# RWKV scan in 64x64 blocks: each head's own 64 columns, on the diagonal quarters of the array

## Chip, core and metric

The program runs on one core of a Trainium2 chip. The metric is the device time of one launch in microseconds. The inputs and outputs are float32, and so is all arithmetic in the part that the change touches.

## What is computed

The program is a two-layer trunk over 256 context tokens and 1024 latent tokens of width 1024. The change is in the first layer's RWKV mixer: 8 heads of 64 channels, scanned over the tokens in both directions, context first.

```python
def delta_scan(s0, seq, dr, reverse):
    '''S <- S diag(w) - (S kk)(kk*a)^T + v k^T ; y = S r.  S: (B,H,Nv,Nk).'''
    def step(s, inp):
        r_t, w_t, k_t, v_t, kk_t, a_t = inp
        s_kk = jnp.einsum('bhvk,bhk->bhv', s, kk_t)
        s = (s * w_t[:, :, None, :] - s_kk[..., None] * (kk_t * a_t)[:, :, None, :]
             + v_t[..., None] * k_t[:, :, None, :])
        return s, jnp.einsum('bhvk,bhk->bhv', s, r_t)
    s_last, ys = lax.scan(step, s0, xs, reverse=reverse)
...
for dr, reverse in enumerate((False, True)):
    s_ctx, yc = delta_scan(s0, ctx, dr, reverse)
    _, yl = delta_scan(s_ctx, lat, dr, reverse)
```

## The kernel before

The 1280 tokens are cut into 20 chunks of 64, and the scan is done chunk by chunk. Inside a chunk the recurrence is a triangular system, whose 64x64 inverse is built by doubling: five levels, each of a product, a copy, a second product and a correction. Between chunks a 64x64 state per head is carried.

`rwkv_scan_phase` runs once for each pair of heads (j = 0 to 3). A pair fills the 128 partitions: head 0 in partitions 0 to 63, head 1 in 64 to 127. The inverse's matrices are kept 128 by 128, one block per head on the diagonal and zeros off it, so that one 128x128 product serves both heads; the cross terms that the products of keys leave are masked by `tri`. Some operands hold the two heads in flipped halves (`vflip`, and `BK` for head 1), so that one 128-row product gathers what it needs from an off-diagonal block. An operand `KR` holds kappa and r of each head beside zeros for the other head.

A pair has 10 rounds and a closing one. Round m does two things at once: it builds the inverses of its two chunks g = 0, 1 in both directions dr (`inv`), and it carries the state through the two chunks of round m-1 (`seq`). The order of the work on each engine is written out by hand. On TensorE (lines 1879 to 1916) it is: `turn_rows` (transposes of the keys, L1839), `right(0)`, `first_inverse` (L1848), `solve(0)`, `level_a(1)`, `outputs(0)`, `level_b(1)`, `level_a(2)`, `right(1)`, `level_b(2)`, `level_a(3)`, `solve(1)`, `level_b(3)`, `level_a(4)`, `outputs(1)`, `level_b(4)`, `level_a(5)`, `products(m+1)` (L1927, the keys' products of the next round), `level_b(5)`. `level_a(l)` is, for each g and dr, a transpose of X (L1863) and a product (L1866); `level_b(l)` is one product each (L1876). Between them VectorE copies Z (L2055) and corrects X (L2063), and ScalarE copies Y (L1955).

In pairs 0 to 2 `PairPrep` computes the next pair's keys in the same rounds: products L1486 to L1502 on TensorE, `unit_key`, `shift` and `scans` on VectorE, `keys` and `rows` on GpSimd, and tables and copies on ScalarE. The last pair has none of it.

SyncE issues all transfers. `stage(m)` loads a round's keys: for j over 0 three transfers per chunk and direction (L1716, L1717), for j = 0 five (L1721 to L1724). `BK` has one buffer, so that `stage(m)` waits for the transposes of round m-1; `KR` has three.

```python
sp.dma_start(KR[hp, m % 3, g, dr, :, h * CK:(h + 1) * CK], kb[j, dr, e, hp, 0:2, :]).then_inc(kr_in[g], 16)
sp.dma_start(BK[:, g, dr, :, :], kb[j, dr, e, :, 2:4, :]).then_inc(bk_in[g], 16)
...
nc.tensor.transpose(bankY[g][:, dr * P:(dr + 1) * P], X[:, g, dr, :], ident[:, :])
x = nc.tensor.matmul(to, Bm[:, g, dr, l, :], X[:, g, dr, :], start=True, stop=True)
```

Of the kernel before, what the change touches and what calls it, by code (L numbers as in the profile page):

```python
# [1395 lines left out]
class PairPrep:  # L1396
# [226 lines left out]
    def rows(self, pool, m):  # L1623
# [21 lines left out]
def rwkv_scan_phase(nc, sems, j, d, kr, bk, kb, last, vtok, srk, lora, projT, yout):  # L1645
# [7 lines left out]
    with ExitStack() as ctx:  # L1653
        s = Scope(nc, ctx, sems, f"rs{j}")
        ident, levels = s.sb("ident", [P, P]), s.sb("levels", [P, 6, P])
        tri, first = s.sb("tri", [P, 2, 2, 2, P]), s.sb("first", [P, 2, 2, P])
        BK = s.sb("BK", [P, 2, 2, 2, CK])
        KR = s.sb("KR", [P, 3, 2, 2, 2, P])
        vflip = s.sb("vflip", [P, NCK, HD])
        gm = s.sb("gm", [P, 2, 2, 2, 2, 2, P])  # L1660
# [40 lines left out]
        with nc.Block() as block:  # L1701
            @block.sync
            def _(sp):
                def stage(m):
# [1477 lines left out]
```

## Time and profile before

| | |
|---|---|
| median of 3 runs | 5291.36 us (5290.5 to 5294.35) |
| profiled execution, its own time | 5289.93 us |
| its span in the trace | 5288.0 us |
| four scans of head pairs, from 880 to about 2131 us | 331, 325, 326 and 269 us |
| in the third pair (1536 to 1862 us) busy: TensorE, VectorE, ScalarE, GpSimd | 255, 202, 144, 126 us |
| in the last pair (1862 to 2131 us) busy: the same | 228, 149, 74, 52 us |
| all that comes before and after the scans | 880 and 3157 us |

The scans take 1251 us of the span, and the change touches nothing else. Within a pair the rounds repeat: from the second on they are 27.9 us apart in pairs 0 to 2 and 23.7 us in the last one. A float32 product stands in the trace as two records of TensorE and two of its weight loads, a transpose as one of each.

### The profile page before, as it was taken

The numbers are of one execution on the slowest core, as the hardware profiler recorded it, in microseconds if no ns is written. First come the engines' busy times: TensorE is split into PE (matmuls) and PEld (weight loads), VectorE is DVE, ScalarE is ACT, GpSimd is POOL, SyncE is SP. The second block draws the span as 40 slices with busy tenths as digits, with TensorE's granted clock in tenths as the row PEclk, the third lists the DMA queues.
The fourth block names the chain that finished last, engine by engine and source line by source line (L and its number), as shares of the span: only waits on it lengthen the run. The fifth ranks groups of instructions, "written<-read, shape, count | busy, mean of one in ns | idle before, by whom it ended". The sixth has DMA issues, their size and how long they took to land. (4 is left out here: it accounts for less than half of the span.)

```text
span 5288.0 us, 69064 instructions
## 1 busy us (share of the span) xinstructions
PE 4090.6 (77%) x23906; PEld 2744.6 (52%) x23907; DVE 2109.5 (40%) x4441; ACT 1455.8 (28%) x3296; POOL 716.9 (14%) x1002
## 2 busy tenths in 40 slices
PE   4998982886868879285799994499899764799973
PEld 2886761775757878172233331389566452233321
DVE  3314545774747655525000002542577534000003
ACT  2213542553435523102111110211466511111111
POOL 0000000343434421301000001010000011000001
PEclk7999995998989989596899997699999886899996
DMA  7211001112111110327868997421300122478996
GB/s 288 71 67 46 8 17 45 44 40 58 48 50 43 38 48 17 115 99 252 310 255 310 375 396 290 159 92 61 129 10 11 55 82 92 184 307 342 394 427 228
DMA packets 292547, 780.17 MB, mean 148 GB/s; under 512 B 114276, under 2 KB 203128, under 8 KB 261592
## 3 DMA queue, kind: packets, MB, share of 16 engines
q1 hardware_dynamic: 239032, 645.96, 33.2%
q10 hardware_dynamic: 38736, 82.33, 4.1%
q0 software_dynamic: 14544, 48.79, 2.5%
q8 instruction: 143, 2.34, 0.2%
q14 instruction: 92, 0.75, 0.1%
HBM read 651.51 MB, written 117.60 MB: 145 GB/s over the span
## 5 line engine op out<-in xcount | busy, mean ns | idle before, releaser
L2862 PE MATMUL ex_bY<-ex_w,ex_aT 128*64 x880 | 389.1, 595 | 73.7 <-DVE ex_aT L2925 73.7
L2862 PE MATMUL ex_bG<-ex_w,ex_xT 128*64 x880 | 404.6, 614 | 39.3 <-SPq L2783 25.8
L2865 PE MATMUL ex_bG<-ex_w,ex_xT 128*64 128x512 f32 x880 | 404.6, 614 | 0.0
L2865 PE MATMUL ex_bY<-ex_w,ex_aT 128*64 128x512 f32 x880 | 389.4, 595 | 0.0
L2865 PE MATMUL ex_bU<-ex_w,ex_xT 128*64 128x512 f32 x880 | 386.6, 592 | 0.0
L2862 PE MATMUL ex_bU<-ex_w,ex_xT 128*64 x880 | 386.6, 592 | 0.0
L2923 DVE TENSOR_TENSOR ex_a<-ex_sg,ex_bU 128x512 f32<-128x512 f32 x55 | 37.8, 688 | 808.0 <-PE ex_bU L2865 808.0
L2862 PEld LDWEIGHTS ex_bG<-ex_w,ex_xT 128*64 128x64 f32 x880 | 123.9, 142 | 302.0 <-issue 302.0
L2862 PEld LDWEIGHTS ex_bY<-ex_w,ex_aT 128*64 128x64 f32 x880 | 116.0, 137 | 299.8 <-issue 299.8
L1022 DVE TENSOR_SCALAR_CACHE_REDUCE ad_p<-ad_S 128x512 f32<-128x512 f32 (+1 forms) x384 | 215.7, 600 | 100.5 <-PE ad_S L944 100.5
L2862 PEld LDWEIGHTS ex_bU<-ex_w,ex_xT 128*64 128x64 f32 x880 | 120.6, 137 | 247.5 <-issue 247.5
L1866 PE MATMUL rs_bankZ<-rs_X,rs_Bm 128*128 128x128 f32 x1280 | 225.3, 277 | 0.0
L1863 PE MATMUL rs_bankY<-rs_ident,rs_X 128*128 128x128 f32 x640 | 185.3, 289 | 43.5 <-DVE rs_Bm L2081 37.8
L1778 POOL TENSOR_TENSOR rs_Bm<-rs_gm,rs_levels 128x384 f32<-128x384 f32 x160 | 157.2, 1004 | 427.9 <-DVE rs_gm L2049 425.0
L1876 PE MATMUL rs_bankY<-rs_Z,rs_Y 128*128 128x128 f32 x1280 | 185.9, 288 | 37.2 <-DVE rs_Z L2055 37.1
L2896 ACT ACTIVATE ex_xT<-ex_tr 128x512 f32<-128x512 f32 x114 | 62.1, 594 | 546.4 <-PE ex_tr L2847 546.4
L2929 DVE COPY ex_y<-ex_bY 128x512 f32<-128x512 f32 x55 | 38.0, 692 | 434.4 <-PE ex_bY L2865 434.4
L1955 ACT ACTIVATE rs_Y<-rs_bankY 128x256 f32<-128x256 f32 x320 | 122.9, 384 | 318.2 <-PE rs_bankZ L1866 318.2
L944 PE MATMUL ad_S<-ad_K,ad_q 64*128 64x512 f32 (+1 forms) x768 | 193.6, 584 | 17.2 <-DMA ad_lqk<-in_od_lk 13.0
L1866 PEld LDWEIGHTS rs_bankZ<-rs_X,rs_Bm 128*128 128x128 f32 x1280 | 205.0, 200 | 0.0
L2063 DVE TENSOR_TENSOR rs_X<-rs_X,rs_bankY 128x256 f32<-128x256 f32 x320 | 134.3, 421 | 169.8 <-PE rs_bankY L1876 166.1
L969 PE MATMUL ad_acc<-ad_V,ad_pT 128*128 128x128 f32 x1280 | 186.9, 285 | 17.9 <-ACT ad_pT L1093 17.9
(435 smaller groups left out, 9736.1 us busy)
## 6 DMA issues: line engine op xcount, KB each, us to landing
ex_w<-in_moe_w_gate SPq DMA_DIRECT2D x64, 2048.0 KB, 11.8
ex_w<-in_moe_w_up SPq DMA_DIRECT2D x64, 2048.0 KB, 16.1
ex_w<-in_moe_w_down SPq DMA_DIRECT2D x64, 2048.0 KB, 15.3
yb_dram<-ex_y ACTq DMA_DIRECT2D x55, 512.0 KB
rt_mw<-in_mod_w SPq DMA_DIRECT2D x24, 1024.0 KB, 9.0
n_mw<-in_mod_w SPq DMA_DIRECT2D x16, 1024.0 KB, 7.5
kb_dram<-rs_pout SPq DMA_DIRECT2D x60, 256.0 KB, 2.5
p_w<-in_od_w_in SPq DMA_DIRECT2D x12, 1024.0 KB, 5.0
```

The lines of the kernel that those rows point to most:

```text
L944: x = nc.tensor.matmul(S[j % 2][c][:, 0:w], q[h, pair, t * P - q_from:(t + 1) * P - q_from], K[h, kmap(pair), a:a + w], start=True, stop=True)
L969: x = nc.tensor.matmul(acc[m % 2][:, c * HD:c * HD + VW], pT[:, g % 3, k * P:(k + 1) * P], V[:, kt, vc:vc + VW], start=kt == 0, stop=kt == ...
L1022: nc.vector.tensor_scalar(p[:, u, c, a:a + w], S[j % 2][c][:, 0:w], scale, None, ALU.mult, ALU.max, accum_out=top[:, u, c, i:i + 1]).then_ ...
L1778: x = nc.gpsimd.tensor_tensor(Bm[:, g, dr, 3:6, :], gm[:, par, g, dr, 0, 0:1, :].to_broadcast([P, 3, P]), levels[:, 3:6, :], ALU.mult)
L1863: nc.tensor.transpose(bankY[g][:, dr * P:(dr + 1) * P], X[:, g, dr, :], ident[:, :])
L1866: x = nc.tensor.matmul(to, Bm[:, g, dr, l, :], X[:, g, dr, :], start=True, stop=True)
L1876: x = nc.tensor.matmul(bankY[g][:, 256 + dr * P:256 + (dr + 1) * P], a[:, g, dr, :], b[:, g, dr, :], start=True, stop=True)
L1955: aa.did(f"X{g}" if l == 1 else f"Y{l}{g}", nc.scalar.activation(to[:, g, :, :], bankY[g][:, 0:256].rearrange("p (d t) -> p d t", d=2), AC ...
L2063: va.did(f"X{l}{g}", nc.vector.tensor_tensor(X[:, g, :, :], X[:, g, :, :], corr, ALU.subtract))
L2862: nc.tensor.matmul(bank[0:BR, :], stationary[:, k, 0:BR], w[:, ds(slot0 + (offset + k * n), 512)], start=k == 0, stop=k == tiles - 1)
L2865: m = nc.tensor.matmul(bank[BR:P, :], stationary[:, k, BR:P], w[:, at:at + 512], start=k == 0, stop=k == tiles - 1)
L2896: nc.scalar.activation(xT[:, 4 * b:4 * b + 4, :], tr[b][:, :].rearrange("p (k t) -> p k t", k=4), ACT.Copy).then_inc(xT_done, 1)
```

## The change

Each head now keeps only its own 64 columns. All matrices of the inverse are 64 columns wide over 128 partitions, one head above the other, and no zeros are stored. Each product is made of two halves, which stand on the diagonal quarters of the array: head 0 reads partitions 0 to 63 and writes PSUM partitions 0 to 63, head 1 reads and writes 64 to 127. The transposes become products with a unit matrix `eye`, two halves each; the transposes of the keys take four halves per chunk and direction instead of one instruction (beta and key apart, beta by minus `eye`). The element-wise operations on VectorE, ScalarE and GpSimd go over half the columns, and the masking operation over 512 in place of 1024. The flipped layouts go: `KR` and `BK` become one tile `KB` with three buffers, loaded by one transfer per chunk and direction (for j = 0 by two), and the first `stage` stands ahead of the constants. The memsets of `KR` and `btm` go. ScalarE's four half-partition operations per chunk after the transposes become one, and four half-partition operations of `rows` on GpSimd become two.

```diff
@@ PairPrep.rows
-        for h in range(2):
-            pool.wait_ge(self.parts, n + 1 + 2 * h)
-            g.tensor_tensor(self.out[h * HD:(h + 1) * HD, :, :, 2 + h, :], chunks(self.be, h), chunks(self.inv, h), ALU.mult).then_inc(self.parts, 1)
-            g.tensor_tensor(self.out[h * HD:(h + 1) * HD, :, :, 3 - h, :], chunks(self.kd, h), chunks(self.inv, h), ALU.mult).then_inc(self.parts, 1)
+        g.tensor_tensor(self.out[:, :, :, 2, :], chunks(self.be), chunks(self.inv), ALU.mult).then_inc(self.parts, 1)
+        g.tensor_tensor(self.out[:, :, :, 3, :], chunks(self.kd), chunks(self.inv), ALU.mult).then_inc(self.parts, 1)
@@ rwkv_scan_phase
-        KR = s.sb("KR", [P, 3, 2, 2, 2, P])
+        KB = s.sb("KB", [P, 3, 2, 2, 4, CK])
...
-        X, Y, Z = (s.sb(n, [P, 2, 2, P]) for n in "XYZ")
+        X, Y, Z = (s.sb(n, [P, 2, 2, HD]) for n in "XYZ")
@@ stage
+                    if m >= 3:
+                        pb.wait(sp, "d11", m - 3)
                     for g in GS:
-                        if m:
-                            pa.wait(sp, f"T{g}", m - 1)
-                        if m >= 3:
-                            pb.wait(sp, "d11", m - 3)
...
-                                sp.dma_start(BK[:, g, dr, :, :], kb[j, dr, e, :, 2:4, :]).then_inc(bk_in[g], 16)
+                                sp.dma_start(KB[:, m % 3, g, dr, :, :], kb[j, dr, e, :, :, :]).then_inc(kb_in[g][m % 3], 16)
...
+                stage(0)
+                for t, n in ((ident, "ident"), (levels, "levels"), (eye, "eye"), (tri, "tri"), (first, "first")):
                     sp.dma_start(t[:], d[n]).then_inc(c_in, 16)
-                sp.wait_ge(kr_clear, 1)
-                stage(0)
@@ TensorE
+                def halves(out, left, right, start=True, stop=True):
+
+                    for hp in HALVES:
+                        x = nc.tensor.matmul(out[hp], left[hp], right[hp], start=start, stop=stop)
+                    return x
...
-                            nc.tensor.matmul(bankS[dr][:, 0:HD], KR[:, q3, c, dr, 0, :], S[:, dr, :], start=True, stop=False)
+                            halves(bankS[dr][:, 0:HD], KB[:, q3, c, dr, 0, :], S[:, dr, :], stop=False)
...
-                                x = nc.tensor.transpose(bankY[g][:, dr * P:(dr + 1) * P], BK[:, g, dr, :, :].rearrange("p a t -> p (a t)"), ident[:, :])
+                                for a in range(2):
+                                    x = halves(bankY[g][:, (2 * dr + a) * HD:(2 * dr + a + 1) * HD], KB[:, m % 3, g, dr, 2 + a, :], eye[:, 1 - a, :])
...
-                                    nc.tensor.transpose(bankY[g][:, dr * P:(dr + 1) * P], X[:, g, dr, :], ident[:, :])
+                                    halves(bankY[g][:, dr * HD:(dr + 1) * HD], X[:, g, dr, :], eye[:, 0, :])
...
-                            x = nc.tensor.matmul(bankZ[g][:, dr * 256:(dr + 1) * 256], BK[:, g, dr, :, :].rearrange("p a t -> p (a t)"), KR[:, m % 3, g, dr, :, :], start=True, stop=True)
+                            for a in range(2):
+                                x = halves(bankZ[g][:, (2 * dr + a) * P:(2 * dr + a + 1) * P], KB[:, m % 3, g, dr, 2 + a, :], KB[:, m % 3, g, dr, 0:2, :].rearrange("p k t -> p (k t)"))
@@ ScalarE
-                            for h in range(2):
-                                hp, other = slice(h * HD, (h + 1) * HD), slice((1 - h) * HD, (2 - h) * HD)
-                                nc.scalar.activation(btm[hp, par, g, :, 0, hp], T[hp, :, hp], ACT.Copy, scale=-1.0)
-                                x = nc.scalar.activation(btm[hp, par, g, :, 1, other], T[hp, :, other], ACT.Copy)
-                            aa.did(f"bt{g}", x)
+                            aa.did(f"bt{g}", nc.scalar.activation(btm[:, par, g, :, :, :], bankY[g][:, 0:256].rearrange("p (d a t) -> p d a t", d=2, a=2), ACT.Copy))
@@ VectorE
-                nc.vector.memset(KR[:, :, :, :, :, :], 0.0).then_inc(kr_clear, 1)
...
-                        pair = bankZ[g][:, :].rearrange("p (k o t) -> p k o t", o=1, t=P).to_broadcast([P, 4, 2, P])
-                        va.did(f"gm{g}", nc.vector.tensor_tensor(gm[:, par, g, :, :, :, :].rearrange("p a b c t -> p (a b) c t"), pair,
-                                                                 tri[:, :, :, :, :].rearrange("p a b c t -> p (a b) c t"), ALU.mult))
+                        va.did(f"gm{g}", nc.vector.tensor_tensor(gm[:, par, g, :, :, :, :].rearrange("p a b c t -> p (a b c t)"), bankZ[g][:, :],
+                                                                 tri[:, :, :, :, :].rearrange("p a b c t -> p (a b c t)"), ALU.mult))
```

The remaining products of `right`, `solve`, `outputs` and the levels change in the same way, from one call of `matmul` to one of `halves`.

TensorE, second pair (rs1), one level of round 0: `level_b(1)` and `level_a(2)` of the kernel before. bankY and bankZ are the PSUM banks of chunk g, ident is the unit matrix.

```order
L1876 MATMUL rs1_bankY0<-rs1_Z,rs1_Y 128x128 x2
L1876 MATMUL rs1_bankY1<-rs1_Z,rs1_Y 128x128 x2
L1863 MATMUL rs1_bankY0<-rs1_ident,rs1_X 128x128
L1866 MATMUL rs1_bankZ0<-rs1_X,rs1_Bm 128x128
L1863 MATMUL rs1_bankY0<-rs1_ident,rs1_X 128x128
L1866 MATMUL rs1_bankZ0<-rs1_X,rs1_Bm 128x128
L1863 MATMUL rs1_bankY1<-rs1_ident,rs1_X 128x128
L1866 MATMUL rs1_bankZ1<-rs1_X,rs1_Bm 128x128
L1863 MATMUL rs1_bankY1<-rs1_ident,rs1_X 128x128
L1866 MATMUL rs1_bankZ1<-rs1_X,rs1_Bm 128x128
```

The same place after the change; all of them now stand under the line of `halves`, L1778.

```order
L1778 MATMUL rs1_bankY0<-rs1_Z,rs1_Y 64x64 x4
L1778 MATMUL rs1_bankY1<-rs1_Z,rs1_Y 64x64 x4
L1778 MATMUL rs1_bankY0<-rs1_eye,rs1_X 64x64 x2
L1778 MATMUL rs1_bankZ0<-rs1_X,rs1_Bm 64x64 x2
L1778 MATMUL rs1_bankY0<-rs1_eye,rs1_X 64x64 x2
L1778 MATMUL rs1_bankZ0<-rs1_X,rs1_Bm 64x64 x2
L1778 MATMUL rs1_bankY1<-rs1_eye,rs1_X 64x64 x2
L1778 MATMUL rs1_bankZ1<-rs1_X,rs1_Bm 64x64 x2
L1778 MATMUL rs1_bankY1<-rs1_eye,rs1_X 64x64 x2
L1778 MATMUL rs1_bankZ1<-rs1_X,rs1_Bm 64x64 x2
```

The order of the steps is the same; each instruction became two, of head 0 and then of head 1.

SyncE's queue at the start of the second pair, before the change.

```order
L1726 DMA rs1_ident<-in_ident 128x128
L1726 DMA rs1_levels<-in_levels 128x768
L1726 DMA rs1_tri<-in_tri 128x1024
L1726 DMA rs1_first<-in_first 128x512
L1716 DMA rs1_KR<-kb_dram 64x2x64 x2
L1717 DMA rs1_BK<-kb_dram 128x128
...
L1731 DMA rs1_vflip<-vtok 64x10x64 x4
```

And after it.

```order
L1709 DMA rs1_KB<-kb_dram 128x256 x4
L1715 DMA rs1_ident<-in_ident 128x128
L1715 DMA rs1_levels<-in_levels 128x384
L1715 DMA rs1_eye<-in_eye 128x128
L1715 DMA rs1_tri<-in_tri 128x512
L1715 DMA rs1_first<-in_first 128x256
L1718 DMA rs1_vch<-vtok 64x10x64 x4
```

The keys' transfers went from twelve (the pattern of three stands four times) to four, and moved ahead of the constants, which went from four to five; the 19 transfers of the preparation's constants follow in both.

## Rows read from the trace of the kernel before

**Rows 1.** Windows: length, PE, PEld, DVE, ACT, POOL busy, clock, DMA share, GB/s.
```profile
1645.70:1673.60 27.90, 24.18 (x191) 22.16 (x191) 19.74 (x47) 14.39 (x48) 12.11 (x20) 1.00 0.17 46
2064.70:2088.40 23.70, 22.08 (x177) 20.37 (x177) 14.32 (x35) 7.37 (x30) 5.01 (x8) 1.00 0.10 24
```

**Rows 2.** Timeline, third pair, TensorE: T, levels 2 to 5, products, next T.
```profile
1645.73 0.89 PE L1839 MATMUL rs_bankY<-rs_ident,rs_BK 128*128 128x128 f32 x4
...
1653.93 0.33 PE L1863 MATMUL rs_bankY<-rs_ident,rs_X 128*128 128x128 f32 x1 [0.85 <-DVE rs_Bm L2081]
...
1658.25 0.33 PE L1863 MATMUL rs_bankY<-rs_ident,rs_X 128*128 128x128 f32 x1
...
1662.21 0.33 PE L1863 MATMUL rs_bankY<-rs_ident,rs_X 128*128 128x128 f32 x1
...
1667.42 0.31 PE L1863 MATMUL rs_bankY<-rs_ident,rs_X 128*128 128x128 f32 x1
...
1669.81 1.97 PE L1927 MATMUL rs_bankZ<-rs_KR,rs_BK 128*128 128x256 f32 x8 [0.86 <-DVE rs_Z L2055]
...
1673.63 0.44 PE L1839 MATMUL rs_bankY<-rs_ident,rs_BK 128*128 128x128 f32 x2
```

**Rows 3.** Timeline, last pair, TensorE: T, level 2, level 4, level 5.
```profile
2064.67 0.89 PE L1839 MATMUL rs_bankY<-rs_ident,rs_BK 128*128 128x128 f32 x4
...
2072.87 0.33 PE L1863 MATMUL rs_bankY<-rs_ident,rs_X 128*128 128x128 f32 x1 [0.85 <-DVE rs_Bm L2081]
...
2079.23 0.33 PE L1863 MATMUL rs_bankY<-rs_ident,rs_X 128*128 128x128 f32 x1
...
2083.97 0.33 PE L1863 MATMUL rs_bankY<-rs_ident,rs_X 128*128 128x128 f32 x1
```

**Rows 4.** Timeline, TensorE without waits: transposes and products of level 4, then outputs(1).
```profile
1662.60 0.27 PE L1863 MATMUL rs_bankY<-rs_ident,rs_X 128*128 128x128 f32 x1
...
1662.93 0.27 PE L1863 MATMUL rs_bankY<-rs_ident,rs_X 128*128 128x128 f32 x1
...
1664.88 0.39 PE L1830 MATMUL rs_bankS<-rs_vflip,rs_btm 128*128 128x64 f32 x2
...
1665.55 0.39 PE L1831 MATMUL rs_bankS<-rs_U,rs_btm 128*128 128x64 f32 x2
```

**Rows 5.** Timeline, TensorE: scores on two row halves; experts on two column halves.
```profile
4002.27 1.13 PE L944 MATMUL ad_S<-ad_K,ad_q 64*128 64x512 f32 x4
...
2701.82 0.59 PE L2862 MATMUL ex_bG<-ex_w,ex_xT 128*64 x1
2701.84 0.59 PE L2865 MATMUL ex_bG<-ex_w,ex_xT 128*64 128x512 f32 x1
2702.25 0.59 PE L2862 MATMUL ex_bG<-ex_w,ex_xT 128*64 x1
```

**Rows 6.** Weight loads by source (min/median/max ns) and group (mean ns); ten router transposes.
```profile
L2590 PEld LDWEIGHTS rt_bankL<-rt_ident,rt_lgT x18: 135/139/142, 2450.9 to 4451.9; 36*128 36x128 f32 x18
...
L2862 PEld LDWEIGHTS ex_bY<-ex_w,ex_aT 128*64 128x64 f32 x880 | 116.0, 137 | 299.8 <-issue 299.8
...
2450.94 0.78 PE L2590 MATMUL rt_bankL<-rt_ident,rt_lgT 36*128 36x36 f32 x10 [0.56 <-ACT rt_lgT L2610]
```

**Rows 7.** VectorE groups of the third pair; the two scans of one round.
```profile
L2063 DVE TENSOR_TENSOR rs_X<-rs_X,rs_bankY 128x256 f32<-128x256 f32 x64 | 26.9, 421 | 35.4 <-PE rs_bankY L1876 34.6
...
L2049 DVE TENSOR_TENSOR rs_gm<-rs_bankZ,rs_tri 128x1024 f32<-128x1024 f32 x16 | 19.4, 1213 | 0.0
...
1667.71 1.25 DVE L1590 TENSOR_TENSOR_SCAN rs_pcum<-rs_prestart,rs_psga 128x128 f32<-128x128 f32 x2
```

**Rows 8.** Timeline, start of the third pair: SyncE's first and last constant, TensorE's next.
```profile
1536.13 0.35 SPq L1726 DMA_DIRECT2D rs_ident<-in_ident  x1
...
1560.36 0.33 SPq L1460 DMA_DIRECT2D rs_pind<-in_headcols  x1
...
1562.29 2.07 PE L1486 MATMUL rs_bankP<-lora,rs_pwl 128*128 128x128 f32 x8 [11.46 <-DMA rs_pind<-in_headcols]
```

**Rows 9.** Windows, router logits: 36 of 128 columns of the array; columns as in Rows 1.
```profile
2431.00:2450.00 19.00, 19.00 (x48) 5.55 (x46) 0.00 (x0) 1.18 (x2) 0.00 (x0) 0.88 0.59 230
```

More of the change, by code:

```diff
@@ L1805, in right @@
                                 va.wait(pe, "X51", m - 1)
[L1806 to L1807 removed]
+                            halves(bankS[dr][:, 0:HD], KB[:, q3, c, dr, 0, :], S[:, dr, :], stop=False)
+                            pb.did(f"R{c}{dr}", halves(bankS[dr][:, 0:HD], gm[:, q, c, dr, 1, 0, :], vch[:, e, :], start=False))
                     def solve(c):
@@ L1811, in solve @@
                             ab.wait(pe, f"R{c}{dr}", m - 1)
-                            pb.did(f"U{c}{dr}", nc.tensor.matmul(bankS[dr][:, HD:2 * HD], Yf[:, q, c, dr, :], R[:, dr, :], start=True, stop=True))
+                            pb.did(f"U{c}{dr}", halves(bankS[dr][:, HD:2 * HD], Yf[:, q, c, dr, :], R[:, dr, :]))
                     def outputs(c):
@@ L1847, in first_inverse @@
                             for dr in DIRS:
-                                x = nc.tensor.transpose(bankY[g][:, dr * P:(dr + 1) * P], Y[:, g, dr, :], ident[:, :])
+                                x = halves(bankY[g][:, dr * HD:(dr + 1) * HD], Y[:, g, dr, :], eye[:, 0, :])
                             pa.did(f"X{g}", x)
@@ L1862, in level_a @@
                                 if l > 1:
-                                    nc.tensor.transpose(bankY[g][:, dr * P:(dr + 1) * P], X[:, g, dr, :], ident[:, :])
-                                to = bankY[g][:, 256 + dr * P:256 + (dr + 1) * P] if l == 1 else bankZ[g][:, dr * P:(dr + 1) * P]
-                                x = nc.tensor.matmul(to, Bm[:, g, dr, l, :], X[:, g, dr, :], start=True, stop=True)
+                                    halves(bankY[g][:, dr * HD:(dr + 1) * HD], X[:, g, dr, :], eye[:, 0, :])
+                                to = bankY[g][:, 256 + dr * HD:256 + (dr + 1) * HD] if l == 1 else bankZ[g][:, dr * HD:(dr + 1) * HD]
+                                x = halves(to, Bm[:, g, dr, l, :], X[:, g, dr, :])
                             pa.did(f"L{l}a{g}", x)
@@ L1875, in level_b @@
                                 a, b = (Z, Y) if l == 5 else (Y, Z)
-                                x = nc.tensor.matmul(bankY[g][:, 256 + dr * P:256 + (dr + 1) * P], a[:, g, dr, :], b[:, g, dr, :], start=True, stop=True)
+                                x = halves(bankY[g][:, 256 + dr * HD:256 + (dr + 1) * HD], a[:, g, dr, :], b[:, g, dr, :])
                             pa.did(f"L{l}b{g}", x)
@@ L3041, in _ @@
                     act.wait_ge(x_out[u], 16 * rounds)
-CONSTS = ("cos", "sin", "ident", "ones", "blockones", "headones", "headcols", "tri", "first", "levels", "before", "iota", "tokid", "desc")
+CONSTS = ("cos", "sin", "ident", "ones", "blockones", "headones", "headcols", "tri", "first", "levels", "eye", "before", "iota", "tokid", "desc")
 def build(nc, d, out):
```

101 lines of the change are left out of this document (44 added, 57 removed).

## Prediction

> **What bounds the kernel now.** I read the windows of the four scans first, then one round of the third and of the last pair on the timeline, then TensorE's rows where it does not wait. In a round TensorE is busy 24.2 of 27.9 us, in the last pair 22.1 of 23.7, at the full clock; VectorE is next with 19.7 and 14.3 [rows 1]. TensorE's cost per product is read where nothing waits [rows 4]: from L1830 at 1664.88 to L1831 at 1665.55 lie three products, 0.223 us each; from one L1863 to the next lie 0.33 us for a transpose and a product, so a transpose takes 0.11. The products there have 64 and 128 moving columns and cost the same. What they share is the 128 columns of weights, loaded twice: the weight load sets this pace.
>
> One round without preparation holds 72 such products, 24 transposes and 4 wide products (L1927: 1.97 us for four, 0.445 each [rows 2]): 16.1 + 2.6 + 1.8 = 20.5 us. The round takes 23.7, so 3.2 us are waits for VectorE and ScalarE. The preparation adds six products and a transpose that nothing else feeds, and two narrow ones, 1.7 us together: 22.2 of 27.9, with 5.7 us of waits. VectorE's preparation (reciprocal, shifts, scans) makes most of that difference.
>
> **The price of a pair of halves, p.** Everything hangs on what two 64x64 halves cost together. No row shows halves that differ in rows and in columns at once. Two neighbours exist [rows 5]. The attention scores use two row halves: four records of 512 moving columns end after 1.13 us, and one such record takes 0.43 (next sentence), so four in a row would take 1.7; they run side by side. The experts use two column halves: the second starts 0.02 us after the first, and the couple repeats every 0.43. So I take the diagonal halves to run side by side too. Each then loads 64 columns twice. A load of 64 columns lasts 137 ns, as the router's transposing load does (139), and ten of those transposes follow each other in (0.78 - 0.22) / 9 = 0.062 us, with 0.22 for the last one by the narrow matmul's length [rows 6]. Hence p = 2 x 0.062 = 0.125 us. The lower end is half of 0.223, 0.112: half the columns. The upper ends: 0.223 if the halves take turns at half the load each, and 4 x 0.062 = 0.25 if the router's 0.062 is no load but the pace at which a load and its matmul can enter. I take 0.125 because the two neighbours ran side by side and because the router's load is the one that 137 ns matches.
>
> **TensorE's work after.** The 72 products become 72 pairs, 20 of the transposes become 20 pairs of full products, the four of the keys become 8 pairs: 100 pairs, 12.5 us. The wide products become 8 pairs with 128 moving columns, bound by these at 0.223: 1.8. Sum 14.3 against 20.5. A transpose gets slightly dearer (0.125 against 0.11).
>
> **VectorE.** An operation on 256 columns takes 0.42, on 1024 1.21 [rows 7]: 0.00103 us a column, so 128 columns take 0.29 and 512 take 0.69. The two large masks give back 1.0 us a round, the others half a dozen tenths each level. GpSimd and ScalarE get shorter as well; they are at 12 and 14 of 27.9 us [rows 1], and I count nothing for them.
>
> **The round, by segments,** each TensorE's work plus what is left, before and after. Last pair [rows 3]; T is the start of `turn_rows`:
> T to level 2: 24 products and 8 transposes, 6.2 of 8.2 us; left 2.0, of which three VectorE operations on the way (two corrections and a mask) are 1.3. After: 36 pairs 4.5, three operations 0.9, 0.6 left: 6.0.
> Level 2 to 4: 22 products and 8 transposes, 5.8 of 6.4. After: 30 pairs 3.75. The hand-overs that the longer stream covered come out: product, copy, product, correction is a chain of about 2.0 us a level even at half the width. I put 4.5.
> Level 4 to 5: 18 products, 4 transposes, 4.5 of 4.7. After 22 pairs 2.75 and 0.35: 3.1.
> Level 5 to next T: 8 products, 4 transposes, the wide ones: 4.0 of 4.4. After 1.5 + 1.8 + 0.4: 3.7.
> Sum 17.3 against 23.7, a gain of 6.4.
> With preparation [rows 2]: T to level 2 8.2, after 6.2 (VectorE shares its port with a busier GpSimd). Level 2 to 4: 8.3, after 7.0, since the reciprocal and the shifts keep their length and are no longer covered. Level 4 to 5: 5.2, after 3.8. To the products: 2.4, set by VectorE's scans (1.25 for two [rows 7]) and the state; it stays 2.4. Products to T: 3.8, stays, as the wide products, the preparation's four and the hand-over remain. Sum 23.2 against 27.9, a gain of 4.7.
> Thirty rounds of 4.7 are 141 us, ten of 6.4 are 64.
>
> **Heads and tails.** At a pair's start TensorE stands until SyncE's last constant: 24.2 us for 39 transfers, 0.62 each [rows 8]. After it there are 32, 4.3 us less, and the wait for the memset of `KR` goes: 5 us in three pairs; in the first 47 become 36: 7. Sum 22. In the closing round the 32 products of `seq` save 32 x 0.098 = 3.1, four times 12. `KB` with three buffers removes a wait of SyncE that ends a round ahead of its use: nothing.
>
> Sum 141 + 64 + 12 + 22 = 239 us. The profiled execution took 5289.9, the median 5291.4, so I predict 5050 us. With p = 0.112 each round loses 1.3 us more: 4998.
>
> **Where the skill speaks against it.** The neighbours of rows 5 either write to two banks (the scores) or read the same rows (the experts); the halves here do neither. The Trainium skill, "TensorEngine Tiling (Array Packing)", Restrictions and Gotchas, says that different row tiles "cannot access same PSUM bank simultaneously". By that rule the halves take turns, which is rival 1 below. No run so far shows two row halves in one bank. And the router's 0.062 us may be an entry pace: the Trainium skill, "TensorE: Matmul & The Clock Gate", Wait — 56ns, not 53.3ns?, gives about 62 ns per matmul where the sequencer's microcode decodes it. That would make a pair 0.25 us.
>
> **Rivals.**
> 1. The halves take turns, or enter too slowly: p = 0.223. For it: no row has two row halves in one bank; the router's equal 0.062 us fits an entry pace too. Against: both neighbours. TensorE's round becomes 22.3 + 3.6 = 25.9 us, 27.6 with preparation; waits shrink to 2.0 and 3.5, since VectorE is faster: 27.9 and 31.1, slower by 4.2 and 3.2. That is 42 + 96 - 22 for the heads = 116 slower: 5405. It decides from p of about 0.2 on: 40 rounds with some 80 of the 100 pairs on the path turn 239 us into nothing at 0.075 more. Chance 10%.
> 2. Side by side, but the hand-overs decide: rounds of 25.5 and 20.0. For it: 3.2 and 5.7 us of waits stand already, and VectorE has 19.7 of 27.9 [rows 1]. Against: its work shrinks too, to about 15. Gain 30 x 2.4 + 10 x 3.7 + 34 = 143: 5147. Chance 15%.
> 3. The array half filled loses the full clock, and everything on TensorE doubles: some 34 and 30.6 us, 5290 + 183 + 69 - 34 = 5508. Against it: the router's logits fill 36 of 128 columns for 19 us at a mean granted clock of 0.88 [rows 9], with the full level in most of it. Chance 3%.
> That the change does nothing: 1%; the line of `halves` stands in the program.
>
> **Numbers.** My forecast has 71%, nearly all of it between 4985 and 5100. The range of 4985 to 5180 takes in the lower price of p and most of rival 2, and leaves out rivals 1 and 3 and a few per cent at the edges. A measurement of this kernel tells 0.2%, 11 us, from no change. Faster: the forecast and rival 2, 86%; same 1%; slower 13%.
>
> **What would show it.** In the profile after: two records of head 0 and head 1 starting within 0.02 us of each other; pairs of 64x64 products every 0.125 us where nothing waits; VectorE's mask at 0.69 and its corrections at 0.29 us; rounds 23 and 17 us apart; the first L1486 of a pair 5 us nearer to its start; the clock at 1.00 in a round. The prediction is wrong if the halves start one after the other, if the records keep 0.11 us each, or if the clock in the rounds falls to 0.5.

## The result, and the profile after

The changed kernel takes 4986.35 us (median of 4 runs, 4979.65 to 4993.97), the kernel before in the same comparison 5292.51 us (4 runs, 5290.5 to 5294.35): a ratio of 0.9422, 95% interval 0.9406 to 0.9438, 306 us less. The forecast was 5050, its range 4985 to 5180: right in sign and in mechanism, and 64 us too careful. The result lies 1.4 us inside the lower end of the range, and the interval of the measurement (4978 to 4995 us) reaches across that end: that it fell inside is luck. The profiled execution took 4985.55 us, its span is 4983.8.

First the windows of one round of the third and of one of the last pair, columns as in rows 1, to be held against these.

```profile
1469.60:1491.00 21.40, 17.54 (x447) 16.09 (x447) 14.69 (x47) 12.31 (x42) 8.96 (x18) 1.00 0.21 62
1774.10:1790.30 16.20, 15.02 (x432) 14.18 (x432) 9.39 (x35) 5.39 (x24) 3.36 (x8) 1.00 0.01 4
```

Rounds are 21.4 and 16.3 us apart instead of 27.9 and 23.7; TensorE is busy 17.5 and 15.0 us, VectorE 14.7 and 9.4. TensorE issues more than twice as many instructions and is still done sooner; in the last pair it is now busy 93% of the round. The granted clock is 1.00 in both.

The same rounds on the timeline, TensorE: T (the start of `turn_rows`), levels 2 to 5, wide products, next T, for [rows 2]; then T, levels 2, 4 and 5, the wide products and the next T of the last pair, for [rows 3].

```profile
1469.63 1.15 PE L1778 MATMUL rs_bankY<-rs_eye,rs_KB 64*64 64x64 f32 x32 [0.16 <-DVE rs_Yf L2043]
...
1474.97 0.33 PE L1778 MATMUL rs_bankY<-rs_eye,rs_X 64*64 64x64 f32 x4 [0.72 <-DVE rs_Bm L2063]
...
1478.64 0.33 PE L1778 MATMUL rs_bankY<-rs_eye,rs_X 64*64 64x64 f32 x4 [0.16 <-DVE rs_X L2045]
...
1481.75 0.33 PE L1778 MATMUL rs_bankY<-rs_eye,rs_X 64*64 64x64 f32 x4 [0.16 <-DVE rs_X L2045]
...
1485.29 0.33 PE L1778 MATMUL rs_bankY<-rs_eye,rs_X 64*64 64x64 f32 x4
...
1487.18 1.96 PE L1778 MATMUL rs_bankZ<-rs_KB 64*64 64x128 f32 x32 [0.74 <-DVE rs_Z L2037]
...
1491.00 1.15 PE L1778 MATMUL rs_bankY<-rs_eye,rs_KB 64*64 64x64 f32 x32 [0.16 <-DVE rs_Yf L2043]
...
1774.06 1.15 PE L1778 MATMUL rs_bankY<-rs_eye,rs_KB 64*64 64x64 f32 x32
...
1779.40 0.33 PE L1778 MATMUL rs_bankY<-rs_eye,rs_X 64*64 64x64 f32 x4 [0.72 <-DVE rs_Bm L2063]
...
1783.65 0.33 PE L1778 MATMUL rs_bankY<-rs_eye,rs_X 64*64 64x64 f32 x4
...
1786.59 0.33 PE L1778 MATMUL rs_bankY<-rs_eye,rs_X 64*64 64x64 f32 x4 [0.16 <-DVE rs_X L2045]
...
1787.75 1.96 PE L1778 MATMUL rs_bankZ<-rs_KB 64*64 64x128 f32 x32
...
1790.33 0.86 PE L1778 MATMUL rs_bankY<-rs_eye,rs_KB 64*64 64x64 f32 x22
```

A group of x4 is one pair of halves: each half leaves two records. Between the state's products, where nothing waits, such groups follow each other every 0.117 us (third pair again):

```profile
1483.43 0.28 PE L1778 MATMUL rs_bankS<-rs_vch,rs_btm 64*64 64x64 f32 x4
1483.55 0.28 PE L1778 MATMUL rs_bankS<-rs_U,rs_btm 64*64 64x64 f32 x4
1483.67 0.28 PE L1778 MATMUL rs_bankS<-rs_vch,rs_btm 64*64 64x64 f32 x4
1483.78 0.28 PE L1778 MATMUL rs_bankS<-rs_U,rs_btm 64*64 64x64 f32 x4
```

In [rows 4] one whole product took 0.223. Within such a group the trace has two records that start 0.006 us apart, and the other two 0.058 us later: the two halves go in side by side, as the prediction's first sign asked.

Behind the first transposes a wait is gone. Before the change, `first_inverse` waited for ScalarE's copies of the turned keys (`btm`, eight half-partition operations in a round); after it there are two operations, and TensorE runs through. Before, then after:

```profile
1648.19 0.41 PE L1848 MATMUL rs_bankY<-rs_ident,rs_Y 128*128 128x128 f32 x2 [0.50 <-ACT rs_btm L1968]
...
1471.08 0.72 PE L1778 MATMUL rs_bankY<-rs_eye,rs_Y 64*64 64x64 f32 x16
```

VectorE and GpSimd, groups of the third pair, for [rows 7]:

```profile
L2045 DVE TENSOR_TENSOR rs_X<-rs_X,rs_bankY 128x128 f32<-128x128 f32 x80 | 20.9, 287 | 21.9 <-PE rs_bankY L1778 21.8
...
L2031 DVE TENSOR_TENSOR rs_gm<-rs_bankZ,rs_tri 128x512 f32<-128x512 f32 x20 | 13.6, 680 | 0.0
...
L2063 DVE TENSOR_TENSOR rs_Bm<-rs_gm,rs_levels 128x128 f32<-128x128 f32 x20 | 11.4, 610 | 0.0
...
L1764 POOL TENSOR_TENSOR rs_Bm<-rs_gm,rs_levels 128x192 f32<-128x192 f32 x40 | 22.8, 591 | 90.3 <-DVE rs_gm L2031 90.3
```

The correction fell from 421 to 287 ns, the wide mask from 1213 to 680, as forecast. GpSimd's level masks fell from 1004 to 591 ns and ScalarE's `btm` copies from 1.8 us a round to 0.8, which the prediction counted at nothing.

**Where the 306 us lie.** From the first T of a pair to its tenth: 247.5, 247.9, 249.0 and 211.0 us before, 188.8, 188.4, 189.0 and 144.6 after: 245 less. From the last T of a pair to the first of the next (the tenth round, the closing round, the next head): 77.4, 77.2, 64.2 before, 62.0, 61.5, 47.9 after: 47 less. Ahead of the first T: 6 less. Behind the last: 6 less, of which the scans' own end gives 10.8, up to the first product of the next phase, while the unchanged rest took 4.6 us longer in this execution. Together that is 304, the difference of the two profiled executions.

### The profile page after: what moved, and what is told of

The parts are those of the page before. It is cut to its first block and busy times, and to the rows that moved or that the text cites. A ratio compares the mean times of both kernels' runs of the same rounds, so it can differ in the third digit from the quotient of the medians.

```text
span 4983.8 us, 88788 instructions
## 1 busy us (share of the span) xinstructions
PE 3815.9 (77%) x34146; PEld 2502.8 (50%) x34147; DVE 1896.4 (38%) x4437; ACT 1370.7 (28%) x3056; POOL 597.8 (12%) x938
## 5 line engine op out<-in xcount | busy, mean ns | idle before, releaser
L1778 PE MATMUL rs_bankY<-rs_eye,rs_X 64*64 64x64 f32 x2560 | 168.5, 225 | 42.9 <-DVE rs_Bm L2063 29.9
L484 PE MATMUL p_acc<-hT,p_wh 128*128 128x512 f32 (+1 forms) x480 | 175.2, 365 | 13.7 <-DVE p_wl L499 13.7
L969 PEld LDWEIGHTS ad_acc<-ad_V,ad_pT 128*128 128x128 f32 x1280 | 158.2, 192 | 53.7 <-ACT ad_pT L1093 33.5
L1022 DVE TENSOR_SCALAR_CACHE_REDUCE al_p<-al_S,rq 128x512 f32<-128x512 f32 (+1 forms) x208 | 126.3, 646 | 143.2 <-PE al_S L944 143.2
L969 PE MATMUL al_acc<-V,al_pT 128*128 128x64 f32 x1344 | 171.7, 275 | 10.4 <-ACT al_pT L1093 10.4
L1071 ACT ACTIVATE ad_p<-ad_p,ad_nmax 128x1280 f32<-128x1280 f32 x128 | 173.4, 1355 | 6.0 <-DVE ad_nmax L1027 6.0
L969 PEld LDWEIGHTS al_acc<-V,al_pT 128*128 128x128 f32 x1344 | 163.1, 192 | 23.0 <-ACT al_pT L1093 23.0
```

The source lines that it names most:

```text
L484: mm = nc.tensor.matmul(acc[u % 2][c][:, 0:n], a[:, u // 2, k, at], b[:, k, t0:t0 + n], start=k == 0 and x == 0, stop=k == KT - 1 and x == 2)
L969: x = nc.tensor.matmul(acc[m % 2][:, c * HD:c * HD + VW], pT[:, g % 3, k * P:(k + 1) * P], V[:, kt, vc:vc + VW], start=kt == 0, stop=kt == ...
L1022: nc.vector.tensor_scalar(p[:, u, c, a:a + w], S[j % 2][c][:, 0:w], scale, None, ALU.mult, ALU.max, accum_out=top[:, u, c, i:i + 1]).then_ ...
L1071: nc.scalar.activation(p[:, u, c, 0:W], p[:, u, c, 0:W], ACT.Exp, bias=nmax[:, u, c:c + 1], accum_out=total[:, u, c:c + 1]).then_inc(p_don ...
L1778: x = nc.tensor.matmul(out[hp], left[hp], right[hp], start=start, stop=stop)
```

## The experiments

All are changes of the changed kernel. "Against before" is the ratio to the kernel before on the same chip; T to T is the distance of rounds in the third and in the last pair. Each ratio is known to about 0.0016, so a difference of two of them, given below as "by the ratios", is known to about 12 us; what is smaller rests on the distances of the rounds in the traces, which in the changed kernel repeat to 0.02 us. The cuts of code are condensed.

| kernel | median us | against before, 95% | T to T |
|---|---|---|---|
| before | 5292.5 | 1 | 27.9 / 23.7 |
| changed | 4986.4 | 0.9422 (0.9406, 0.9438) | 21.4 / 16.3 |
| products twice | 5206.4 | 0.9827 (0.981, 0.9843) | 26.6 / 23.2 |
| old widths | 5183.8 | 0.9789 (0.9773, 0.9806) | 27.3 / 20.4 |
| both | 5286.8 | 0.9983 (0.9973, 0.9992) | 28.8 / 24.1 |
| old widths, filled | 5146.1 | 0.9733 (0.9717, 0.9749) | 25.1 to 26.6 / 20.0 |
| GpSimd wide | 5003.0 | 0.9462 (0.9447, 0.9478) | 21.9 / 16.9 |
| many transfers | 5003.3 | 0.9462 (0.9446, 0.9478) | 21.4 / 16.3 |
| mask first | 4959.4 | 0.9377 (0.9361, 0.9393) | 20.8 / 15.8 |
| preparation spread | 4927.0 | 0.9316 (0.93, 0.9331) | 19.3 / 16.3 |
| two queues | 4957.8 | 0.9377 (0.9362, 0.9393) | 21.4 / 16.3 |
| all three | 4892.8 | 0.9253 (0.9237, 0.9268) | 19.2 / 15.8 |
| finer | 4889.8 | 0.9243 (0.9228, 0.9258) | 18.8 / 15.8 |

**1. What a pair of halves costs.** Behind the last round twelve streams are appended on TensorE, 40 pairs or 40 single products each (one run, 5049 us with the streams in it):

```diff
+for _ in range(40):
+    mm(b0[lo, 0:HD], e[lo], e[lo]); mm(b0[hi, 0:HD], e[hi], e[hi])
+for _ in range(40):
+    mm(b0[lo, 0:HD], e[lo], e[lo])
...
```

> The changed kernel with twelve streams of products appended on TensorE after the last pair's last round, each closed by a semaphore; their results go nowhere. Theory (halves run side by side, the columns of weights set the pace): two diagonal halves in one bank repeat every 0.117 us; the same with two banks too; one half alone every 0.117 / 2 = 0.058 to 0.117 us: 0.117 shows the halves overlapping, 0.058 shows that they merely queue at half the cost each. 128 moving columns 0.22 to 0.25 a pair, 32 moving columns still 0.117, 32 columns of weights near 0.06 to 0.08 if the load sets the pace. A full 128x128 product 0.223. Rival (halves take turns at 64 columns of load each): one half alone is exactly half of a pair, and runs of two or four halves of one head cost the same as halves in turn; by the theory of overlap, runs of four of one head cost up to twice as much.

The timeline of this run, TensorE, one row a stream: diagonal halves in one bank; one half alone; halves on the same rows; diagonal halves in two banks; different rows, same columns, two banks; whole products; 128 rows with 64 columns of weights; diagonal halves with 128 moving columns; with 32; with 32 columns of weights; in runs of two of one head; in runs of four.

```profile
1809.23 4.86 PE L1933 MATMUL rs_bankY<-rs_eye 64*64 64x64 f32 x160
1814.15 4.88 PE L1933 MATMUL rs_bankY<-rs_eye 64*64 64x64 f32 x80
1819.08 4.88 PE L1933 MATMUL rs_bankY<-rs_eye 64*64 64x64 f32 x160
1824.03 4.88 PE L1933 MATMUL rs_bankY<-rs_eye 64*64 64x64 f32 x160
1828.98 4.88 PE L1933 MATMUL rs_bankY<-rs_eye 64*64 64x64 f32 x160
1833.93 9.14 PE L1933 MATMUL rs_bankZ<-rs_ident 128*128 128x64 f32 x80
1843.13 4.88 PE L1933 MATMUL rs_bankZ<-rs_ident 128*64 128x64 f32 x80
1848.07 8.95 PE L1933 MATMUL rs_bankY<-rs_first,rs_eye 64*64 64x128 f32 x160
1857.09 4.86 PE L1933 MATMUL rs_bankY<-rs_eye 64*64 64x32 f32 x160
1862.01 4.66 PE L1933 MATMUL rs_bankY<-rs_eye 64*32 64x64 f32 x160
1866.73 4.93 PE L1933 MATMUL rs_bankY<-rs_eye 64*64 64x64 f32 x160
1871.72 6.14 PE L1933 MATMUL rs_bankY<-rs_eye 64*64 64x64 f32 x160
```

Forty pairs take 4.86 us and forty single halves 4.88: with 64 moving columns the second half is free. The records of a single half start every 0.058 us; in the pairs two records start in each 0.058 us. Less the last product's 0.22 that is (4.86 - 0.22) / 39.75 = 0.117 a pair. One bank or two, same rows or other rows: no difference. A product of 128 rows with 64 columns of weights also takes 0.117, a whole one 0.223, so the rows don't count, and from 128 to 64 the time goes with the columns of weights. Below 64 it does not: 32 columns still take 0.112. With 128 moving columns a pair takes 0.22; a single half was not tried there. Halves must alternate at least every other product: runs of two cost 0.118 a pair, runs of four 0.149. A window of the first stream, columns as in rows 1, has the full clock:

```profile
1809.00:1814.00 5.00, 5.00 (x175) 4.95 (x170) 1.92 (x3) 0.34 (x2) 0.00 (x0) 1.00 0.27 59
```

The theory holds, except that 32 columns were expected at 0.06 to 0.08. What bounds them is open.

**2. TensorE's share.** Each pair of products once more, transposes and wide products single:

```diff
 def halves(out, left, right, start=True, stop=True, again=1):
+    for _ in range(again if start else 0):
+        for hp in HALVES:
+            nc.tensor.matmul(out[hp], left[hp], right[hp], start=True, stop=True)
     for hp in HALVES:
```

> Each of the 72 pairs of products of a round is issued once more ahead of itself (for a group that accumulates, its first pair is repeated as often as the group has members), the 28 transposes and the wide products stay single: 72 x 0.117 = 8.4 us more on TensorE in a round, about what the kernel before had. Theory (TensorE's cheaper pairs gave most of the gain): rounds back to about 23.7 in the last pair and 27.5 with preparation, closing rounds 3.7 longer each: 30 x 6.1 + 10 x 7.4 + 15 = 270 more, about 5255. Rival (the narrower element-wise work gave most of it): much of the added work falls into waits, rounds grow by 3 to 4: 5110 to 5150.

5206: 214 us come back by the ratios ((0.9827 - 0.9422) x 5292), between the two expectations. The last pair went to 23.2, nearly the old 23.7; with preparation it went up 5.2 of the 6.5.

**3. The widths' share.** Every element-wise operation of the solve reads and writes its columns twice, for example:

```diff
-Z = s.sb("Z", [P, 2, 2, HD])
+Z = s.sb("Z", [P, 2, 2, 2, HD])
...
-nc.vector.tensor_copy(Z[:, g, :, :], at)
+nc.vector.tensor_copy(Z[:, g, :, :, :], twice(at))
```

> TensorE as in the changed kernel, but every VectorE, ScalarE and GpSimd operation of the solve reads and writes each column twice, so that it has the widths of the kernel before (256 and 1024 columns instead of 128 and 512). Theory: 1.0 us a round in the last pair and 2 with preparation come back, 30 x 2 + 10 x 1 = 70: about 5055. Rival (the element-wise work gave most of the gain): 150 or more come back, 5140 or above.

5184: 194 us come back, where 70 were expected; that is the rival's range. Round by round the trace gives the reason; stretches of one round of the third pair, columns as in rows 1:

```profile
1668.70:1672.00 3.30, 3.25 (x92) 2.98 (x94) 3.23 (x8) 2.50 (x10) 0.00 (x0) 1.00 0.00 0
1672.00:1675.60 3.60, 1.72 (x60) 1.58 (x56) 3.60 (x8) 2.73 (x7) 3.16 (x4) 1.00 0.02 5
1675.60:1678.00 2.40, 1.86 (x48) 1.68 (x48) 2.37 (x6) 0.90 (x4) 1.76 (x2) 0.93 0.00 0
1678.00:1681.00 3.00, 1.84 (x30) 1.51 (x28) 2.50 (x7) 0.27 (x2) 2.11 (x6) 0.50 0.00 0
1681.00:1684.00 3.00, 2.22 (x44) 2.03 (x42) 2.81 (x6) 1.44 (x5) 2.37 (x5) 0.50 0.02 5
1684.00:1688.00 4.00, 3.90 (x75) 3.71 (x73) 2.31 (x6) 0.77 (x2) 0.00 (x0) 0.51 0.14 39
1688.00:1692.00 4.00, 2.88 (x73) 2.65 (x69) 3.17 (x9) 2.29 (x8) 1.27 (x3) 1.00 0.80 243
```

VectorE is busy in nearly all of 1672 to 1678, while TensorE waits for 2.4 of these 6 us; from 1678 to 1688 TensorE's granted clock is 0.50, the lower of its two levels (1.2 GHz). The mean granted clock is 0.79 to 0.81 in every round of this pair. Of the 27 rounds of the first three pairs two stayed at 1.00, and both are 25.1 long instead of 27.3 (one at 0.93 was 25.1 long, too, so a dip needn't cost anything). In the last pair the one round at 1.00 took 19.3, the later ones at 0.92 took 20.4. So some of the 194 us is the widths' own price and some is the clock.

**4. Both.** Experiments 2 and 3 together.

> Both at once: products twice and element-wise work at the old widths. If TensorE's cost, the widths and the transfers are all that changed, it comes back to the time before less heads: 5250 to 5300. If it stays below 5220, something else gave time (the two matters overlap, or the masks and rows on GpSimd).

5287: all of it is back (0.9983), within the expectation. Two things nearly cancel: the rounds take 21 us more in all than before the change, since TensorE's work is dearer than the old one (72 x 0.234 = 16.8 us against 72 x 0.223 = 16.1, and 28 pairs at 0.117 = 3.3 against 24 transposes at 0.11 = 2.6), and the gaps between the pairs and the first head take 25 us less. A round of the third pair:

```profile
1641.00:1669.80 28.80, 25.69 (x735) 24.29 (x735) 20.00 (x47) 13.87 (x42) 10.67 (x18) 1.00 0.16 46
```

But the shares don't add up: with TensorE's change but the old widths (experiment 3) the kernel is 112 us faster than before, with the new widths but the old work of TensorE (experiment 2) 92, with both 306. Each of the two smaller numbers holds some 21 us of the transfers (experiment 7). Part of what is missing is the clock. A round with preparation grows by 5.2 us in experiment 2, by 5.9 in experiment 3 and by 7.4 in this one, where TensorE is busy for 25.7 of 28.8 us and the clock is at 1.00. Of the 3.7 us by which the first two exceed the third, 2.2 are what experiment 3 lost to the clock (27.3 against 25.1); the other 1.5, as I read it, are work that falls into a wait which the other part has made anyway. In the last pair it is 3.2 us, of which 1.1 are the clock.

**5. Work added, time saved.** Experiment 3 with sixteen idle pairs a round. They write to `bankP`, the preparation's bank, and not to one of their own:

```diff
 level_b(1)
+fill(10)
 level_a(2)
...
+fill(6)
 level_b(2)
```

> The run with the old widths (e3_wide) and in addition ten idle pairs of products ahead of level 2 and six ahead of the second product of level 2, on a bank of their own: 1.9 us more of TensorE's work in a round, in places where it waits for VectorE. In e3_wide the granted clock falls to 0.50 for 10 us of each round behind those waits. Theory (the widths cost twice: once as waits, once because TensorE then loses its full clock): the clock stays at 1.00, rounds with preparation come down from 27.3 to about 25.1, the last pair from 20.4 to 19.5, and the time falls by 50 to 70 although work is added: about 5120. Rival (the clock follows something else): rounds as in e3_wide or up to 1.9 us longer, 5184 to 5260.

5146, 30 us less than without the filling by the ratios, though TensorE does 1.9 us a round more; 50 to 70 were expected. The clock stayed at 1.00 in 12 of the 27 rounds of the first three pairs, where it had been 2, and in all nine of the last pair, where it had been one. A round of the third pair in which the clock still dips and the next in which it doesn't, and one of the last pair:

```profile
1544.30:1571.00 26.70, 21.52 (x513) 19.77 (x513) 20.23 (x47) 13.59 (x43) 10.80 (x18) 0.94 0.17 50
1571.00:1596.10 25.10, 19.98 (x513) 18.23 (x513) 20.11 (x47) 13.54 (x43) 10.79 (x18) 1.00 0.19 53
1834.30:1854.40 20.10, 17.70 (x498) 16.39 (x498) 14.97 (x35) 6.51 (x24) 5.14 (x8) 1.00 0.11 29
```

The clock is what experiment 3 lost besides: with it kept, 25.1 and 20.0, the latter with 0.7 us of the filling's own in it. So at full clock the old widths cost 3.7 us a round with preparation (25.1 - 21.4) and 3.0 in the last pair (19.3 - 16.3, experiment 3's own round at 1.00), where the expectation of experiment 3 had 2 and 1. It counted only the operations on the way; that each of them also pushes the next back is my reading, and no run shows it by itself.

**6. GpSimd's share.** Only L1764 has its old width (384 columns), and for that writes to a tile of its own, `Bw`; the rest is the changed kernel.

> Only GpSimd's three masks of a chunk have the old width (384 columns, 1.0 us each instead of 0.57); VectorE, ScalarE and TensorE as in the changed kernel. Theory (GpSimd's operations stretch VectorE's level-2 mask that runs beside them, 1.15 us for two with and 0.62 without, and TensorE waits for it ahead of level 2): about 0.5 to 1 us a round, 20 to 40 in all: 5007 to 5027. Rival (GpSimd has time to spare, nothing on the path, as the prediction counted): within 10 us.

5003, 21 us by the ratios, rounds 0.5 and 0.6 longer: the theory, in size. Two groups of that run, GpSimd's masks and VectorE's level-2 mask beside them (610 ns in the changed kernel), and the row where TensorE pays:

```profile
L1769 POOL TENSOR_TENSOR rs_Bw<-rs_gm,rs_levels 128x384 f32<-128x384 f32 x40 | 39.2, 1010 | 84.7 <-DVE rs_gm L2036 84.7
...
L2068 DVE TENSOR_TENSOR rs_Bm<-rs_gm,rs_levels 128x128 f32<-128x128 f32 x20 | 15.4, 808 | 0.0
...
1488.87 0.33 PE L1783 MATMUL rs_bankY<-rs_eye,rs_X 64*64 64x64 f32 x4 [0.32 <-DVE rs_Bm L2068]
```

VectorE's instruction is the same and takes 0.2 us longer, with nothing changed but the width and the target of what GpSimd does beside it. The place is not quite the one that the theory names: T to level 2 grows by only 0.1 us (5.42 against 5.34), and level 2 to level 4 by 0.4 in the third pair and 0.5 in the last. It is the second chunk's mask that comes late, inside level 2.

**7. The transfers.**

```diff
-sp.dma_start(KB[:, m % 3, g, dr, :, :], kb[j, dr, e, :, :, :])
+for h in range(2):
+    sp.dma_start(KB[HALVES[h], m % 3, g, dr, 0:2, :], kb[j, dr, e, HALVES[h], 0:2, :])
+sp.dma_start(KB[:, m % 3, g, dr, 2:4, :], kb[j, dr, e, :, 2:4, :])
```

In the first pair there are five such transfers, and the first round's stand behind the constants again.

> The loads of the keys as in the kernel before: three transfers a chunk (five in the first pair) instead of one (two), and the first round's behind the constants. Theory: nothing in the rounds; heads 5 us longer in three pairs and 7 in the first at most, so 4986 + 22 = 5008 or less. Rival (transfers matter in the rounds, too): 5030 or more, with TensorE waiting for the keys inside a round.

5003, 21 us. The rounds did not change at all. Last T to next first T went from 62.0, 61.5, 47.9 to 67.2, 66.4, 52.4, and the first T of all is 8.0 later: 5.3 + 4.9 + 4.5 + 8.0 = 22.7. The 8.0 is known to about 2 us: in the runs that leave the first head alone, the first T lies between 906.4 and 908.4. The theory holds, and one transfer a chunk gives nothing else.

**8. A mask ahead of the corrections.**

```diff
 masked(1)
+mask_2(0)
 for g in GS:
     correct(1, g)
-mask_2(0)
 mask_2(1)
```

> VectorE makes the level-2 mask of the first half of the chunks ahead of the two corrections of level 1 instead of behind them, and TensorE starts level 2 there after the first correction. Theory (what is left in a round ahead of level 2 is VectorE's chain, not TensorE): 0.5 us a round, forty rounds, 20 us: 4966. Rival (TensorE then waits at the next hand-over): no change within 5 us.

4959, 24 us by the ratios; 0.6 and 0.5 us a round, all of it between T and level 2 (4.77 instead of 5.34 in the third pair). The wait ahead of level 2 was VectorE's chain. How much of it is the order and how much the masks themselves, which now take 339 ns instead of 610, is not separated.

**9. The preparation spread.**

```diff
-if back: prep.unit_key(dve, m - 1)
-level(2); prep.shift(dve, m, 2); prep.shift(dve, m, 1)
-level(3); prep.shift(dve, m, 0)
-level(4); prep.scans(dve, m)
-state(1); level(5)
+if back: prep.unit_key(dve, m - 1)
+level(2); prep.inverted_norm(dve, m - 1)
+level(3); prep.scaled_key(dve, m - 1); prep.shift(dve, m, 2)
+level(4, between_4); prep.scans(dve, m)
+state(1); level(5, lambda: prep.shift(dve, m, 0))
```

Beyond VectorE's order, ScalarE's square now stands behind its output copies, and TensorE's preparation products wait for two shifts instead of three.

> VectorE's preparation for the next pair is spread over its idle times: reciprocal behind level 2, scaled key and one shift behind level 3, a shift and the gates inside level 4, the last shift inside level 5. Theory (a round with preparation is 5.1 us longer than one without because VectorE's preparation stands ahead of the copies that TensorE waits for): 1.9 us a round, thirty rounds, 57 us: 4930. Rival (GpSimd's or ScalarE's part of the preparation becomes late instead): less than 20 us or slower.

4927, 56 us by the ratios, rounds with preparation 19.3 instead of 21.4. Theory, to the size, for the three changes of order together.

**10. Two queues.** The columns, the ones and the index of heads are issued by ScalarE.

> Fifteen small constants of the preparation are issued from ScalarE's queue beside SyncE's. Theory (a head lasts as long as SyncE needs to issue its transfers): 15 x 0.47 = 7 us less in each of three heads, 21 us: 4965. Rival (the transfers' landing sets it): within 5 us.

4958, 24 us. Last T to next first T fell from 62.0 and 61.5 to 55.5 and 54.6, and the first T of all came 7.1 sooner: 20.4 in the three heads. SyncE's issuing sets the head.

**11. All three, and a finer order.**

> The changed kernel with all three: the level-2 mask ahead of the corrections (28 less by itself), the preparation spread over VectorE's idle times (59 less), fifteen constants on ScalarE's queue (29 less). Theory (they act at different places): they add up, 116 less, about 4870, rounds of 18.7 and 15.8. Rival (mask and preparation fill the same idle time): 4885 to 4900.

4893, ratio 0.9253: 89 us by the ratios. The 116 was a sum of plain medians; by the ratios the three parts are 24, 56 and 24, 104 together. The rounds with preparation are 19.2, hardly less than 19.3 without the mask's change: the expectation failed there, and the rival, with 4885 to 4900, was right. VectorE's copies of level 4 were now late by 0.5 us and TensorE waited 0.59 for ScalarE's square.

> The combined version once more (e9_all, 4893) with the reciprocal inside level 2, key and first shift behind level 2, the second shift behind level 3, the gates inside level 4, and ScalarE's square ahead of its output copies. In e9_all VectorE's copies of level 4 come 0.5 us late and TensorE waits 0.6 us for the square ahead of its preparation products. Theory (these two waits are on the path): 1.0 us a round, thirty rounds, 30 less: 4863, rounds of 18.2. Rival (the closing of a round, wide products and hand-over, sets it): within 8 us of 4893.

4890, rounds of 18.8: 0.4 of the expected 1.0, and the medians of the two can't be told apart. The wait for the square is gone from the trace. A round of 18.77 us in its third pair has TensorE busy for 17.43, at 1.00: 1.3 us are left to waits. These two beat both kernels, by 1.8 and 1.9% of the changed one.

## Why the prediction was right, and where it was short

**The price of a pair** was the step on which all hung: side by side, 0.125, lower end 0.112. It is 0.117 (experiment 1). The way to 0.125, twice the pace of a load of 64 columns, is not a rule that holds further down: 32 columns take 0.112. The upper ends are out: the halves don't take turns (rival 1), and 0.062 was no entry pace for these products: four loads and four matmul records enter in 0.117. TensorE's round was forecast at 14.3; with 100 pairs at 0.117 and the wide ones it is 13.5. That is 0.8 us a round, up to 32 us of the 67 (306 - 239) that were missing, and it is part of each segment below.

**The rule against it.** The Trainium skill, "TensorEngine Tiling (Array Packing)", Restrictions and Gotchas, that different row tiles cannot access the same bank at once, is not borne out in that form: one bank and two banks take 4.86 and 4.88 us. Here the two row tiles write different partitions of the bank. The Trainium skill, "PSUM — Partial Sum Buffer", PSUM bank collisions raise a hardware error, quotes the same broad rule, but what it reports as measured between two row tiles is a collision in the same bank and the same 32 partitions, and the runs here fit that narrower form. Two row halves on the same partitions of one bank were not tried.

**VectorE's sizes** were right (0.29 and 0.69 forecast, 0.287 and 0.680 measured), but two in a row take less than twice one (0.47 to 0.52 for a pair on the timeline), which the segments did not use.

**The segments**, forecast and measured. Third pair: T to level 2 6.2, 5.34; to level 4 7.0, 6.78; to level 5 3.8, 3.54; to the products 2.4, 1.89; to T 3.8, 3.82. Sum 23.2, 21.4. Last pair: 6.0, 5.34; 4.5, 4.25; 3.1, 2.94; 3.7, 3.74. Sum 17.3, 16.3. The pairs that were priced too dear explain 0.3 of the first stretch and nearly all of the next two (0.2 to 0.3 each). Two steps failed beyond that.

The first is T to level 2. There I left 0.6 us, and with preparation 0.8, of waits behind the three operations; measured 5.34 less 36 pairs at 0.117 and the three operations at 0.9 leaves 0.2. The reason given, that VectorE shares its port "with a busier GpSimd", had the wrong sign: GpSimd is busy for 9.0 us of a round instead of 12.1. What had filled most of the rest before was the 0.50 us that `first_inverse` waited for ScalarE's `btm` copies, and it is gone. So "I count nothing for them" was wrong for ScalarE by up to 0.5 us a round in this stretch (read from the traces; no run puts the eight copies back alone), and for GpSimd by 0.5 to 0.6, 21 us in all (experiment 6), in the stretch behind it, where my round numbers for the hand-overs happened to take it in.

The second is "it stays 2.4" between level 5 and the products. VectorE's scans start 0.05 us ahead of level 5 instead of 0.29 behind it, since the correction ahead of them is narrower, and the copy behind them is narrower, too: together 0.5. In all 30 x 1.8 + 10 x 1.0 = 64 us.

**Heads and tails.** The three gaps between pairs gave 47 us: 21 up to the closing rounds' first product, 7 in the closing rounds' products, 19 behind their last. The first head gave 6. So the heads measured 25 against the 22 forecast (in the third pair the first L1486 comes 19.3 us after SyncE's first transfer instead of 26.2). Most of that is the transfers (experiment 7), and part of the rest is the memset of `KR`, for which SyncE had waited 1.6 us (1537.9 to 1539.5 in the kernel before). The closing products gave 1.5, 1.5, 4.3 and 2.4 us, 10 against the 12 forecast; the 4.3 is partly the clock, whose mean over that stretch was 0.61 before the change and 0.78 after it.

**Rival 2**, that hand-overs decide, had a true core that I put at the wrong place. Left as wide as they were, the element-wise operations would have kept the rounds at 27.3 and 20.4 (25.1 and 19.3 where the clock stayed full; experiment 3): of 306 us only 112 would have come. The gain needed both parts: where one of them alone gets shorter, the other sets the end of the same chain, and TensorE's waits then cost it the full clock besides.

**Rival 3**, the loss of the full clock: its reason is refuted (streams of 64x64 halves and the rounds run at 1.00), but its mechanism exists. Experiments 3 and 5 use the same halves of the array as the changed kernel, and there the clock goes down behind TensorE's waits and comes back when the waits are filled. The changed kernel is at 1.00 in all its rounds but the first of each of the pairs 1 to 3.

## What to carry to other kernels

Where products are block-diagonal by 64, issue them as alternating halves on the diagonal quarters: with 64 moving columns the second one is free, and a product of 128 rows with 64 columns of weights costs no more than a quarter does. Narrow the copies and masks between the products in the same step: here either part alone, with the transfers, gave about a third of what both gave. When TensorE's work shrinks and its waits stay, look at its granted clock, and count what a neighbour on the other element-wise engine does to the instruction for which TensorE waits.

## What the runs showed of the hardware that I had not expected

- Forty products of one 64x64 quarter take as long as forty pairs on two quarters (4.88 and 4.86 us).
- A quarter with 32 columns of weights is hardly faster (0.112) than with 64 (0.117), and 32 moving columns cost what 64 do.
- Adding 1.9 us of idle products to each round made a kernel 30 us faster (0.9789 to 0.9733 of before): the granted clock stayed at 1.00 in 21 of 36 rounds instead of 3.
- The same VectorE instruction of 128x128 took 610 ns beside GpSimd's narrow masks, 808 beside its wide ones; moved ahead of the corrections (experiment 8) the first of each two fell mostly into a pause of GpSimd, and the mean was 339. The timeline of the first run of experiment 11 has such a one, between masks of GpSimd that end at 1390.83 and start again at 1391.39:

```profile
1391.22 0.28 DVE L2078 TENSOR_TENSOR rs_Bm<-rs_gm,rs_levels 128x128 f32<-128x128 f32 x1
```
